# Means of squares of q and k: two fp32r products of high and low parts in place of one fp32 product

## The reference

```
q = proj[..., OFF_Q:OFF_K].reshape(bsz, seq, DA_HEADS, 2, DA_QK)
y = xf * lax.rsqrt(jnp.mean(xf * xf, axis=-1, keepdims=True) + EPS)
q = partial_rope(rmsnorm(q, qk_norm_g[l, 0]), cos, sin)
```

## Time and profile before

| | us |
|---|---|
| median of 3 runs | 1321.64 (1320.49 to 1321.82) |
| the profiled execution | 1321.91 |
| its span | 1320.1 |
| TensorE busy | 1299.8 |
| VectorE busy | 852.1 |
| GpSimd busy | 618.3 |
| ScalarE busy | 486.8 |

### The profile page before, as it was taken

How to read it: one execution, slowest core, us unless ns; L and a number is a source line. 1 busy time by engine, 2 the same in 40 slices (tenths; PEclk the granted TensorE clock), 3 DMA queues, 4 the chain that set the end, 5 groups by cost and what they waited for, 6 DMA issues and landing times.

```text
span 1320.1 us, 16016 instructions
## 1 busy us (share of the span) xinstructions
PE 1299.8 (98%) x6234; PEld 1056.6 (80%) x6234; DVE 852.1 (65%) x1149; ACT 486.8 (37%) x742; POOL 618.3 (47%) x288
## 2 busy tenths in 40 slices
PE   7999999999999999999999999999999999999999
PEld 4888777787888888888878887867878888888887
DVE  7789884846888217776237798677477760377721
ACT  6333446644233212223334244476442222122220
POOL 2986452144444434443468764412444444444442
PEclk9999999999999999999999999999999999999999
DMA  5232221023333323333232223201333333233332
GB/s 210 79 107 65 83 92 42 25 85 109 100 100 101 107 86 96 96 96 110 82 110 82 83 65 95 86 18 56 95 106 101 98 104 104 80 97 96 108 110 86
DMA packets 40938, 120.48 MB, mean 91 GB/s; under 512 B 6432, under 2 KB 10656, under 8 KB 40864
## 3 DMA queue, kind: packets, MB, share of 16 engines
q1 hardware_dynamic: 40864, 119.46, 28.9%
HBM read 114.20 MB, written 2.10 MB: 88 GB/s over the span
## 4 chain that ended last, share of the span: by engine, by line
PE 90%; DVE 5%; ACT 2%; POOL 2%; DMA 1%; issue 0%; SPq 0%; POOLq 0%; DVEq 0%
PE bank L493 27%; PE bank L506 27%; PE bank L498 25%; PE bank L495 1%; PE bank L685 1%; PE bank L726 1%; POOL wl L354 1%; DMA raw<-in_w_in 1%; ACT G L1032 1%; DVE G L1517 1%; PE bank L652 1%; PE bank L705 1%; PE bank L715 1%; PE bank L585 1%; PE bank L600 1%; DVE ssum L1145 1%
## 5 line engine op out<-in xcount | busy, mean ns | idle before, releaser
L354 POOL TENSOR_TENSOR wl<-raw,wh 128x1024 fp32r<-128x1024 f32 (+3 forms) x208 | 507.7, 2442 | 660.4 <-ACT wh L861 388.9
L861 ACT ACTIVATE wh<-raw 128x1024 fp32r<-128x1024 f32 (+3 forms) x208 | 218.7, 1052 | 276.3 <-PE bank L498 230.7
L493 PE MATMUL bank<-xl,wh 128*128 128x512 f32 x1152 | 305.1, 403 | 0.0
L506 PE MATMUL bank<-xh,wl 128*128 128x512 f32 x1152 | 286.8, 390 | 0.0
L498 PE MATMUL bank<-xh,wh 128*128 128x512 f32 x1120 | 276.9, 389 | 0.0
L493 PEld LDWEIGHTS bank<-xl,wh 128*128 128x128 f32 x1152 | 214.6, 188 | 56.6 <-issue 13.2
L506 PEld LDWEIGHTS bank<-xh,wl 128*128 128x128 f32 x1152 | 215.2, 188 | 44.2
L498 PEld LDWEIGHTS bank<-xh,wh 128*128 128x128 f32 x1120 | 210.2, 188 | 44.2
L1179 DVE TENSOR_TENSOR x<-x,bank 128x512 f32<-128x512 f32 x64 | 43.9, 686 | 228.5 <-PE bank L506 228.3
L493 PE MATMUL bank<-ml,wh 128*128 128x512 f32 x512 | 137.5, 395 | 0.0
L506 PE MATMUL bank<-mh,wl 128*128 128x512 f32 x512 | 127.5, 389 | 0.0
(11 more groups left out here) (290 smaller groups left out, 1251.7 us busy)
## 6 DMA issues: line engine op xcount, KB each, us to landing
raw<-in_w_gu SPq DMA_DIRECT2D x88, 512.0 KB, 3.5
raw<-in_w_in SPq DMA_DIRECT2D x52, 512.0 KB, 3.7
raw<-in_w_dn SPq DMA_DIRECT2D x32, 704.0 KB, 4.1
raw<-in_w_ol SPq DMA_DIRECT2D x16, 384.0 KB, 3.0
raw<-in_w_oe SPq DMA_DIRECT2D x16, 256.0 KB, 2.6
x<-in_x SPq DMA_DIRECT2D x8, 256.0 KB, 6.4
raw<-in_w_first SPq DMA_DIRECT2D x4, 512.0 KB, 5.1
out_x<-x SPq DMA_DIRECT2D x8, 256.0 KB, 4.5
```

The lines of the kernel that those rows point to most:

```text
L354: tt(wl[:, p, 0:cols], raw[:, p, 0:cols], wh[:, p, 0:cols].bitcast(F32), ALU.subtract).then_inc(wl_full, 1)
L493: mm(bank[b][:, :], wh[:, p, k * P:(k + 1) * P], lo[:, k, :], start=(k == 0), stop=False)
L506: w = mm(bank[b][:, :], wl[:, p, k * P:(k + 1) * P], hi[:, k, :], start=False, stop=(k == K - 1))
L861: fn(wh[:, p, 0:cols], raw[:, p, 0:cols], ACT.Copy).then_inc(wh_full, 1)
```

## The change

ScalarE squares twice: into G[:, 2] in fp32 and into sq_high, an fp32r tile (the rounded square). GpSimd subtracts sq_high from G[:, 2] into sq_low, also fp32r, at steps s = 17 to 24, behind the low part of weight tile s + 1 and, in s = 21, ahead of the imaginary part. TensorE waits for sq_low (semaphore sqk_low) and adds two fp32r products in bank 4. The blocks of ones are copied once into an fp32r tile, block_r, by VectorE. sq_high and sq_low lie over rows of v, which are free at that time.

```diff
--- before.py
+++ after.py
@@ -104,6 +104,7 @@
         xbc = sb("xbc", [P, 6, T], at=offsets["qk"])
         z = sb("z", [P, 2, T], at=offsets["qk"] + 6 * T * 4)
         xbt = sb("xbt", [P, NQ, 4, P], at=offsets["v"])
+        sq_high, sq_low = [sb(f"sqk_{n}", [P, T], F32R, at=offsets["v"] + (2 + i) * T * 4) for i, n in enumerate(("high", "low"))]
         u = sb("u", [P, 2, T])
         pad = sb("pad", [P, 2, 4 + T])
         G = sb("G", [P, 6, T])
@@ -169,6 +170,7 @@
         cst = sb("cst", [P, NCONST])
         rotary = sb("rotary", [P, 2, T])
         cbf = sb("cbf", [P, 2, P], BF16)
+        block_r = sb("block_r", [P, P], F32R)
         s16 = sb("s16", [P, 12, NQ * M2H])
         mlam_all = sb("mlam_all", [P, L])
         soft = sb("soft", [P, 2, 8])
@@ -225,7 +227,9 @@
         em_full, em_high, mixed_ready = sem("em_full"), sem("em_high"), sem("mixed_ready")
 
         partner_in = [sem(f"partner_in{p}") for p in range(2)]
-        sqk_ready, qk_rms, qk_done, v_ready = [sem(n) for n in ("sqk_ready", "qk_rms", "qk_done", "v_ready")]
+        sqk_ready, sqk_low, qk_rms, qk_done, v_ready = [
+            sem(n) for n in ("sqk_ready", "sqk_low", "qk_rms", "qk_done", "v_ready")]
+        block_ready = sem("block_ready")
         exp_go, exp_done, probs_ready, probs_turned = [
             sem(n) for n in ("exp_go", "exp_done", "probs_ready", "probs_turned")]
         head_copied, osq_ready, head_ln, onorm_done = [
@@ -453,6 +457,9 @@
                             state_terms(l, n)
                     if 13 <= s <= 14:
                         table(l, 1, s - 13)
+                    if 17 <= s <= 24:
+                        pool.wait_ge(sqk_ready, nth(sqk_ready))
+                        tt(sq_low[:, :], G[:, 2, :], sq_high[:, :].bitcast(F32), ALU.subtract).then_inc(sqk_low, 1)
                     if s in (15, 21):
                         s5_imaginary(l, (s - 15) // 6)
                 for _ in range(16 + 2 * (2 * FHALF + 8)):
@@ -680,9 +687,12 @@
             def qk_mean(t):
 
 
-                pe.wait_ge(sqk_ready, nth(sqk_ready))
+                pe.wait_ge(sqk_low, nth(sqk_low))
                 claim(4, qk_done)
-                mm(bank[4][:, :], block1, G[:, 2, :], start=True, stop=True).then_inc(act_bank[4], 1)
+                if t == 0:
+                    pe.wait_ge(block_ready, 1)
+                mm(bank[4][:, :], block_r[:, :], sq_high[:, :], start=True, stop=False)
+                mm(bank[4][:, :], block_r[:, :], sq_low[:, :], start=False, stop=True).then_inc(act_bank[4], 1)
 
             def v_turn(l, h):
 
@@ -932,7 +942,8 @@
 
                 def qk_square(t):
                     act.wait_ge(unit_out, unit_out_of(l, 16 + t))
-                    fn(G[:, 2, :], G[:, t % 2, :], ACT.Square).then_inc(sqk_ready, 1)
+                    fn(G[:, 2, :], G[:, t % 2, :], ACT.Square)
+                    fn(sq_high[:, :], G[:, t % 2, :], ACT.Square).then_inc(sqk_ready, 1)
 
                 def s5_copy(i):
 
@@ -1585,6 +1596,7 @@
                     if l == 0 and s == 8:
                         dve.wait_ge(cst_loaded, 16)
                         copy(cbf[:, 0, :], ident)
+                        copy(block_r[:, :], block1).then_inc(block_ready, 1)
                         lambdas()
                     if s == 9:
                         m2_turned(2)
```

## The result

The changed kernel takes 1328.12 us (median of 6 runs, 1326.09 to 1329.63) against 1321.62 (6 runs, 1320.49 to 1321.82): 6.5 us more, ratio 1.005, 95% interval 1.004 to 1.006. The forecast was 1323.0 with a range up to 1326.5, so it is slower than the range allows. The profiled execution is the longest of the six, 1329.63 us (before: 1321.91), its span 1327.9. I read the loss there, and the medians say how large it is as a rule.

A forecast was written before the change was run, and what follows sets the result against it. TensorE, busy 1299.8 of 1320.1 us, was taken as the bound. Means -7.1, wait at the sixth mean +8.1 and copy +0.2 sum to +1.2 us, giving 1323.0 us by the median, range 1320.0 to 1326.5.

The forecast's parts named there:

- rival two: TensorE's clock falls in the new 4 us gap at the sixth mean; 1325.9 us if in one layer; chance 0.10.
- matmuls behind the gap come at more than 0.227 us each: Sign of being wrong: products behind TensorE's wait at the sixth mean run slower than the full pace of 0.227 us.
- two-layer form: Clock falls behind the sixth mean's gap in both layers: 5.7 us on top, 1328.7 us; within a rival given 0.10.
- The comparison with the 9.1 us gap: Argument against a clock fall: the new gap is less than half of TensorE's idle stretch at the start.
- The wait: Sixth mean, step 22: TensorE waits 4.03 us a layer for GpSimd's queued subtract, 8.1 us in both layers.
- TensorE's part: At the 16 means, two fp32r products replace one fp32 product: 0.446 us less each, 7.1 us; period 5.90 us.
- Rival four: The fp32r pair at the means costs TensorE as much as the fp32 product: 1330 us; chance 0.05.
- The ordinary steps: All steps but each layer's sixth: GpSimd's 1.28 us subtract ends 1.4 us before it is wanted; no TensorE wait.
- Rival three: Subtract goes ahead of VectorE's product; next mean waits 1.2 us in some ten steps: 12 us, 1335 us; chance 0.05.
- The copy: First layer: VectorE's copy of the constant block into fp32r, in a stretch TensorE waits for, adds 0.2 us.
- the bad end of 1.4: Worst case for the constant block's copy: one product misses its turn by a GpSimd operation, about 1.4 us.
- Rival one: GpSimd's idle time hides all of its added work, so no wait at the means: 1314.5 us; chance 0.10.

The follow-up runs named there:

- e2_fill16: Changed kernel with 16 fp32r products into unused bank 7 ahead of the sixth mean's wait in both layers; 1324.13 us, ratio 1.0021.
- e6: Changed kernel without GpSimd's subtract, the second product reading sq_high again (sum wrong by that); 1315.28 us, ratio 0.9954 to the kernel before.
- e7: Changed kernel with the sixth subtract behind the imaginary part, ahead of the low half of weight tile 23; 1317.50 us, ratio 0.9969.
- e11: Changed kernel with the S5 output products moved ahead of the sixth mean on TensorE, GpSimd's order unchanged; one run, 1318.82 us.
- e3: Changed kernel with 8 fp32r products into unused bank 7 ahead of the sixth mean's wait in both layers; 1325.72 us, ratio 1.0033.

## Why the prediction was wrong, point by point

**The term that was missing.** The step that failed: the sum priced the wait by its own length and put the products behind it at full pace, with nothing for the clock. The reason stands in rival two: "It decides from a gap that is long enough, and mine is less than half of the one seen." The runs showed a clock at the lower level behind both gaps, and products that took 2.84 and 2.57 us longer, nearly all of it by the clock; "matmuls behind the gap come at more than 0.227 us each" was one of the forecast's own signs of being wrong. I had the mechanism and nearly its price (2.9 us a layer), gave it 0.10, and left its two-layer form (1328.7, measured 1328.12) out of the range. That the price is so near is luck in part: it came from the start of the kernel, where the profile gives a granted clock of 1.000 and x may still have been arriving. The comparison with the 9.1 us gap said nothing: it gave one length behind which the products are slow, not the length from which they are. e2_fill16 shows that the gap is the cause. The sum should have had +5.4 where it had nothing, and with it the changed kernel would have been forecast at 1328.4. That this meets the median is again partly luck: the 5.4 is from the slowest of the six runs, and the small errors below (+0.7 for the means, +0.6 for the v turns, -0.2 for the waits, -0.1 for the copy) would bring the sum to 1329.4, next to that run's 1329.63.

**The wait.** Right: 3.93 and 3.92 us against 4.03, in step 22 alone, for the reason given. The half microsecond of VectorE's product that holds the sixth subtract is there too (1.71 us instead of 1.29).

**TensorE's part.** Mis-sized: 0.40 a mean, not 0.446, so 6.4 us and not 7.1. The period is 5.95, not 5.90: 0.227 x 26 is 5.90, and 0.05 more goes where the mean meets its neighbours (the next unit's first group is busy 2.01 us, not 1.98); why wasn't tested. Rival four is out.

**The ordinary steps.** Right. The subtract takes 1.29 us and starts 3.13 us behind the mean (149.63 - 146.50; forecast 3.1), and no mean but the sixth waits. e6, without any subtract, has the same 5.95 us between its means, so the subtract costs these steps nothing. Rival three is out.

**The v turn.** Not seen: 0.28 us a layer. VectorE is later against TensorE than before, so its last cosine product (198.12, 2.90 us) came behind GpSimd's low half (197.87) where before it had been ahead of it (193.57, the low half at 193.73). e6 loses the same 0.28 us without a subtract, so the subtract isn't the reason:

```profile
193.57 0.74 DVE L1495 SCALAR_TENSOR_TENSOR qk<-G,par_all,rotary 128x512 f32<-128x512 f32 x1
```

```profile
198.12 2.90 DVE L1506 SCALAR_TENSOR_TENSOR qk<-G,par_all,rotary 128x512 f32<-128x512 f32 x1
```

```profile
197.87 2.60 POOL L358 TENSOR_TENSOR wl<-raw,wh 128x1024 fp32r<-128x1024 f32 x1 [1.58 <-PE bank L513]
```

**The copy.** 0.07 us (the wait for xbt is 1.24 us in the timeline before and 1.31 after), forecast 0.2. It went through in 0.21 us, and the cast behind it took 1.29 us where the following product had taken 1.35. The waits stayed, only their place moved; the bad end of 1.4 didn't occur. The copy got in 0.07 us ahead of GpSimd's next operation (80.33 to 81.60). The cast behind it has one SBUF input too and was through only at 81.68, so an operation with one SBUF input is held here too, once GpSimd is first:

```profile
80.26 0.21 DVE L1599 CAST block_r<-cst 128x128 fp32r<-128x128 f32 x1
80.39 1.29 DVE L1347 CAST cbf<-pre 128x128 bf16<-128x128 f32 x1
```

**Rival one** fell by the order of the queue. Its 1314.5 us is what e6 comes near to (1315.3), where there is no subtract at all.

## What to carry to other kernels

A wait in front of a busy TensorE is to be priced twice: its own length, and the slower products behind it if TensorE stands still for some microseconds. Here 3.9 us cost 6.5 to 6.8 a layer. Before giving work to an engine with idle time, write down its queue at the one step where it has least, not in the ordinary step. If a wait can't be avoided, put other work of the waiting engine ahead of it: that alone turned +6.5 us into -3 here.

## What the runs showed of the hardware

Gaps of TensorE and the clock behind them, all in this stage. After 3.78 us it fell to the lower level in both layers of the changed kernel's profile, and its mean was 0.995 to 0.997 in all six runs. After 3.0 us it fell in both layers of a profile, for a shorter time in one, and two runs of four stayed at 0.999. After 1.97 us it fell in one layer and stayed in the other. After 1.03 to 1.12 us it stayed (profiles of e7 and e11; 1.000 in all runs of e7). In the layer of e3 where it fell, it did so only when TensorE had already been at work again for 1.2 us (granted clock 1.00 up to 180.0, 0.50 from 180.1 on; work again from 178.82): the mean's two products took 0.50 and 0.39 us, and the S5 groups behind them 1.30 and then 1.92. The Trainium skill, "TensorE: Matmul & The Clock Gate", Part 1 (The HAM clock gate), says that an idle engine returns to the slow clock. The runs agree in kind; the same gap did and did not lower it, so the gap's length alone doesn't decide, and from which length it is certain stays open.

Products of VectorE with two SBUF inputs were held up by whole operations of GpSimd: 0.74 us alone, up to 2.90 behind one, and two took 4.19 instead of 1.28 behind a pair. What stays open is whether the remaining 1.1 to 1.4 us a layer could be had by another place for the seventh and eighth subtract; I didn't try it.
